# Hybrid decoder step in fp32 on one core: the last recurrent strip in an order of its own, and the first head of each half on a timetable that reaches into the next pass

## What is computed

```python
xn = rmsnorm(x, norm_mix)
xl, gl, q, k, v, z, b_raw, a_raw, u_pool, g_lru, g_dn, g_pool = split_cols(xn @ w_in)
h, h_last = rg_lru(causal_dwconv(xl, ...), ...)             # h[t] = a[t] * h[t-1] + b[t]
o_lru = h * gelu(gl)
o, s_last = gated_delta_rule(qh, kh, vh, beta, g, s0)       # 8 heads of 128, solves (I + A) X = B per chunk
o_dn = rmsnorm(o) * dn_norm_w * silu(z)
o_pool = multiscale_pool(u_pool, ...)
merged = (sigmoid(g_lru) * (o_lru @ w_br_lru) + sigmoid(g_dn) * (o_dn @ w_br_dn)
          + sigmoid(g_pool) * (o_pool @ w_br_pool))
x = x + merged @ w_out
x = x + square(relu(rmsnorm(x, norm_mlp) @ w_up)) @ w_down
```

## Time and profile before

| | |
|---|---|
| median of 3 runs | 2178.59 us |
| lowest, highest | 2177.43, 2178.78 us |
| profiled execution | 2176.55 us |
| its span, first to last instruction | 2174.8 us |
| TensorE busy | 2145.8 us, 99% of the span |
| VectorE, ScalarE, GpSimd busy | 1214.7, 771.8, 180.3 us |
| mean granted TensorE clock | 0.995 |

### The profile page before, as it was taken

The page is one execution under the profiler, slowest core; times in us unless marked ns, Lnnn a source line. Parts: engine busy times, 40 slices in busy tenths (PEclk is TensorE's granted clock), DMA queues, the critical chain, the costliest instruction groups (busy, mean ns, idle before and its releaser), DMA issues.

```text
span 2174.8 us, 34073 instructions
## 1 busy us (share of the span) xinstructions
PE 2145.8 (99%) x14515; PEld 2092.5 (96%) x14515; DVE 1214.7 (56%) x1996; ACT 771.8 (35%) x944; POOL 180.3 (8%) x340
## 2 busy tenths in 40 slices
PE   9999998999999999999999999999999999999997
PEld 9998997999998999999999999999999999999997
DVE  7996885555565655555545554444444444444444
ACT  6334552322232322333333443333333333333333
POOL 7000102110032110020000100000000000000001
PEclk9999999999999999999999999999999999999999
DMA  7443443334443343346444444545454444444443
GB/s 231 148 150 117 145 150 97 118 118 128 125 148 107 119 125 119 108 136 194 154 146 153 148 146 147 154 146 153 148 150 151 148 153 147 154 146 155 146 153 110
DMA packets 295638, 309.40 MB, mean 142 GB/s; under 512 B 9712, under 2 KB 290416, under 8 KB 295232
## 3 DMA queue, kind: packets, MB, share of 16 engines
q1 hardware_dynamic: 291616, 291.54, 43.0%
q0 software_dynamic: 3584, 15.55, 2.4%
q10 hardware_dynamic: 288, 0.15, 0.0%
HBM read 298.83 MB, written 8.37 MB: 141 GB/s over the span
## 4 chain that ended last, share of the span: by engine, by line
PE 88%; DVE 7%; ACT 2%; issue 1%; DMA 1%; SPq 0%; DVEq 0%; ACTq 0%
PE main L1432 27%; PE main L1434 26%; PE main L1433 26%; PE aux L1552 6%; DVE lo L887 2%; DVE scratch L887 2%; DVE scratch L894 1%; ACT hi L621 1%; DVE scratch L891 1%; DMA raw<-in_w_in 1%; PE aux L1525 0%; PE aux L1656 0%; PE aux L1535 0%; DVE qkv L894 0%; DVE merged L887 0%
## 5 line engine op out<-in xcount | busy, mean ns | idle before, releaser
L887 DVE TENSOR_TENSOR lo<-raw,hi 128x1024 fp32r<-128x1024 f32 x546 | 660.4, 1228 | 376.3 <-ACT hi L621 369.0
L1432 PE MATMUL main<-x_hi,hi 128*128 128x320 f32 x2688 | 842.4, 313 | 2.9 <-DVE x_lo L894 2.4
L1434 PE MATMUL main<-x_hi,lo 128*128 128x320 f32 x2688 | 831.4, 309 | 0.0
L1433 PE MATMUL main<-x_lo,hi 128*128 128x320 f32 x2688 | 831.2, 309 | 0.0
L621 ACT ACTIVATE hi<-raw 128x1024 fp32r<-128x1024 f32 x546 | 566.5, 1054 | 688.3 <-DMA raw<-in_w_up 220.4
L1432 PEld LDWEIGHTS main<-x_hi,hi 128*128 128x128 f32 x2688 | 505.5, 188 | 11.0 <-issue 5.0
L1433 PEld LDWEIGHTS main<-x_lo,hi 128*128 128x128 f32 x2688 | 505.6, 188 | 0.7
L1434 PEld LDWEIGHTS main<-x_hi,lo 128*128 128x128 f32 x2688 | 505.1, 188 | 0.0
L1432 PE MATMUL main<-o_hi,hi 128*128 128x320 f32 x1408 | 444.3, 316 | 4.6 <-DVE o_lo L887 4.6
L1434 PE MATMUL main<-o_hi,lo 128*128 128x320 f32 x1408 | 435.7, 309 | 0.0
L1433 PE MATMUL main<-o_lo,hi 128*128 128x320 f32 x1408 | 435.5, 309 | 0.0
(11 more groups left out here) (253 smaller groups left out, 1191.6 us busy)
## 6 DMA issues: line engine op xcount, KB each, us to landing
raw<-in_w_in SPq DMA_DIRECT2D x210, 512.0 KB, 3.5
raw<-in_w_up SPq DMA_DIRECT2D x128, 512.0 KB, 3.7
raw<-in_w_down SPq DMA_DIRECT2D x128, 512.0 KB, 3.4
raw<-in_w_back SPq DMA_DIRECT2D x80, 512.0 KB, 3.4
scratch<-in_s_in POOLq DMA_DIRECT2D x8, 512.0 KB, 4.9
out_s_out<-scratch POOLq DMA_DIRECT2D x8, 512.0 KB, 4.6
merged<-in_x SPq DMA_DIRECT2D x8, 320.0 KB, 7.6
qkv<-in_x POOLq DMA_DIRECT2D x1, 2560.0 KB, 12.4
```

The costliest lines, as they stand in the source:

```text
L887: return dve.tensor_tensor(out, a, b, op)
L1432: pe.matmul(bank, hi, xh, start=first, stop=False)
L1433: pe.matmul(bank, hi, xl, start=False, stop=False)
L1434: return pe.matmul(bank, lo, xh, start=False, stop=last)
```

## The change

Four edits, all in the order of work and in who does it:

1. The chain of strip 3 stands on VectorE behind the split of tile 3 in the order 3, 0, 4, 1, 5, 2, 6 with no split between, and step 7 (the split of the product) one tile later. ScalarE has its steps 0, 3, 1, 4, 2 behind the same tile and step 5 behind tile 5's split. The old step 5 of VectorE is cut in three (5, 6, 7), and the GELU of strip 3 has a buffer of its own (`GQ`).
2. The first head of each half has places of its own for all 19 steps, from tile 5, block 0 to block 3 of tile 0 of the next pass. On VectorE `merge` and `gate` stand at other places among its steps.
3. In every head ScalarE, not VectorE, makes `KBG` (three instructions of 128 columns), and no longer waits for `dn_lt`; VectorE makes `QKD` behind `dn_lt`, not ahead of it.
4. GpSimd prepares the rows of a half's first head ahead of clearing buffers (for head 0 ahead of `o_ready`), and stores `conv_out` earlier. The product of pooling group 3 stands one tile earlier on TensorE, two positions earlier on VectorE and ScalarE.

```diff
+        GQ = (G2, G2, G2, MG[:, 14 * N:16 * N])
...
             def half(h0):
-                rows(h0)
+                ch.link(pool.memset(DTM, 0.0))
+                pool.sem_inc(rm_ready, 1)
                 clear_rows()
...
             pool.wait_ge(row_beg, 2)
-            ch.link(pool.memset(DTM, 0.0))
+            rows(0)
+            pool.wait_ge(o_ready, 4)
             half(0)
...
         def dn_place(k, peeled):
-            if peeled and k < 14:
-                return ((5, 3), (6, 1), (6, 4), (6, 6), (7, 0), (7, 2), (7, 4), (7, 6), (7, 7),
...
+            if peeled:
+                after = (0, 6, 11, 14, 17, 21, 24, 28, 30, 33, 35, 38, 40, 43, 45, 48, 51, 54, 59)[k]
+                return 5 + after // 8, after % 8
...
# ScalarE, dn_step k == 1
-                    act.wait_ge(lt_ready, h + 1)
+                    for c, n in enumerate((P, P, NS)):
+                        act.activation(KBG[0:n, c * P:(c + 1) * P], AX[3][0:n, c * P:(c + 1) * P], ACT.Copy,
+                                       scale=cols(COL, h, 1, c * 56 + 48, 1, n))
...
-            gated(0, GPL_N, GPL_T, 0, lru_steps(lru_step, 3), True)
+            gated(0, GPL_N, GPL_T, 0, {4: [lambda k=k: lru_step(3, k) for k in (0, 3, 1, 4, 2)], 6: [lambda: lru_step(3, 5)]})
...
# VectorE, gated and late
+                    own = {8: [gate0], 9: [dn[0]], 10: [dn[1], dn[2]], 11: [dn[3], merge0, dn[4]], 12: [dn[5], dn[6]]}
...
+                    return {1: [dn[7], dn[8]], 2: [dn[9], dn[10], dn[11]], 3: [dn[12], gate1, dn[13], dn[14]],
+                            4: [dn[16]], 5: [dn[17], merge1, dn[18]]}
...
+            gated(0, GPL_N, GPL_T, 0, 0, 0, {4: [lambda k=k: lru_step(3, k) for k in (3, 0, 4, 1, 5, 2, 6)],
+                                            5: [lambda: lru_step(3, 7)]})
...
# TensorE, gated
+                    for h in (h0, it + h0) if it == 1 else (it + h0,):
+                        for k in range(19):
+                            j, b = dn_place(k, h == h0)
+                            j -= 12 * (it + h0 - h)
+                            if 0 <= j < 12:
+                                between[j] = list(between.get(j, ())) + [(b, lambda h=h, k=k: dn_step(h, k, first))]
...
-            gated(0, GPP_N, GPP_T, 4, 8, 4, {3: [(7, lambda: pool_product(3))]})
+            gated(0, GPP_N, GPP_T, 4, 8, 4, {2: [(7, lambda: pool_product(3))]})
```

More of the change, by code:

```diff
@@ L427, in lru @@
                 history(it + 12, it + 12, it * 2 + 24, it * 4 + (LRU_T + 2 + BANKS))
+                if it == 3:
+                    pool.wait_ge(tail_copied, 16)
+                    pool.dma_start(A["conv_out"], CO).then_inc(out_stored, 16)
                 pool.wait_ge(h_ready, it + 1)
@@ L442, in _ @@
                 lru(it)
-            pool.wait_ge(tail_copied, 16)
+            pool.wait_ge(out_stored, 16)
             pool.wait_ge(lho_copied, 4)
-            pool.dma_start(A["conv_out"], CO).then_inc(out_stored, 16)
             pool.dma_start(A["lru_out"], LHO[:]).then_inc(out_stored, 16)
-            pool.wait_ge(out_stored, 32)
-            pool.wait_ge(o_ready, 4)
             def rows(h):
@@ L456, in rows @@
                                              None, ALU.mult)
-                ins.then_inc(rm_ready, 1)
+                return ins
             def head(h, following):
@@ L468, in head @@
                 if following:
-                    rows(h + 1)
+                    rows(h + 1).then_inc(rm_ready, 1)
                 pool.wait_ge(dn_done, h + 1)
@@ L523, in _ @@
             pool.wait_ge(o_ready, 8)
-            ch.link(pool.memset(DTM, 0.0))
+            rows(4)
             half(4)
@@ L573, in lru_steps @@
             return {pos: [lambda k=k: step(it, k) for k in ks]
-                    for pos, ks in ((3, (0,)), (4, (1,)), (5, (2, 3)), (6, (4,)), (7, (5,)))}
+                    for pos, ks in ((3, (0,)), (4, (1,)), (5, (2, 3)), (6, (4,)), (7, (5, 6, 7)))}
         def qkv_steps(rms, silu, rows):
@@ L597, in dn_place, with dn_steps @@
             return (5 + (k - 6) // 2, (3, 7)[k % 2]) if k < 18 else (11, 6)
-        def dn_steps(step, h, peeled, late):
+        def dn_steps(step, h, late):
             steps = {}
             for k in range(19):
-                pos = dn_place(k, peeled)[0] + 4
+                pos = dn_place(k, False)[0] + 4
                 if (pos > 12) == late:
@@ L769, in dn_step, with gated @@
                     act.activation(S1, AX[2][:, 0:P], ACT.Copy).then_inc(s1_ready, 1)
[L771 to L774, removed]
+            def gated(it, n0, t0, h0, after):
+                if it == 0:
+                    own = {8: [lambda: gate(0, 0, t0, 0)], 10: [lambda: dn_step(h0, 0)], 11: [lambda: dn_step(h0, 1)]}
+                else:
+                    own = joined({8: [lambda: gate(it, 0, t0, 0)]}, dn_steps(dn_step, it + h0, False))
                 walk(split, n0, 12, it, 12, joined(after, own))
             def late(it, t0, h0):
-                steps = {2: [lambda: gate(it, 1, t0, 0)]}
-                return steps if h0 is None else joined(steps, dn_steps(dn_step, it + h0, False, True))
-            gated(0, GPL_N, GPL_T, 0, lru_steps(lru_step, 3), True)
+                if it == 0:
+                    return {3: [lambda: gate(0, 1, t0, 0)], 4: [lambda: dn_step(h0, 15), lambda: dn_step(h0, 16)]}
+                return joined({2: [lambda: gate(it, 1, t0, 0)]}, dn_steps(dn_step, it + h0, True))
+            gated(0, GPL_N, GPL_T, 0, {4: [lambda k=k: lru_step(3, k) for k in (0, 3, 1, 4, 2)], 6: [lambda: lru_step(3, 5)]})
             for it in range(1, 4):
@@ L1196, in dn_step @@
                     tt(XT[0:NS, NP:N], ident[0:NS, 0:NS], YY[0:NS, NP:N], ALU.subtract).then_inc(lt_ready, 1)
+                    for n, c, _ in both:
+                        tt(QKD[0:n, c], AX[1][0:n, c], DTM[0:n, c], ALU.mult)
                 elif k == 2:
@@ L1240, in dn_step, with gated @@
                     ins.then_inc(dn_done, 1)
[L1242 to L1245, removed]
+            def gated(it, n0, t0, g0, h0, branch, after):
+                gate0, merge0 = lambda: gate(n0, t0, it, 0), lambda: merge(n0, t0, g0, it, 0, branch)
+                dn = [lambda k=k: dn_step(h0, k) for k in range(19)]
+                own = {8: [gate0], 10: [merge0]}
+                if h0 is not None and it == 0:
+                    own = {8: [gate0], 9: [dn[0]], 10: [dn[1], dn[2]], 11: [dn[3], merge0, dn[4]], 12: [dn[5], dn[6]]}
+                elif h0 is not None:
+                    own = joined(own, dn_steps(dn_step, it + h0, False))
                 walk(split, n0, 12, it, 12, joined(after, own))
             def late(it, n0, t0, g0, h0, branch):
-                steps = {2: [lambda: gate(n0, t0, it, 1)], 4: [lambda: merge(n0, t0, g0, it, 1, branch)]}
-                return steps if h0 is None else joined(steps, dn_steps(dn_step, it + h0, False, True))
-            gated(0, GPL_N, GPL_T, 0, 0, 0, lru_steps(lru_step, 3), True)
+                gate1, merge1 = lambda: gate(n0, t0, it, 1), lambda: merge(n0, t0, g0, it, 1, branch)
+                dn = [lambda k=k: dn_step(h0, k) for k in range(19)]
+                if h0 is not None and it == 0:
+                    return {1: [dn[7], dn[8]], 2: [dn[9], dn[10], dn[11]], 3: [dn[12], gate1, dn[13], dn[14]],
+                            4: [dn[16]], 5: [dn[17], merge1, dn[18]]}
+                steps = {2: [gate1], 4: [merge1]}
+                return steps if h0 is None else joined(steps, dn_steps(dn_step, it + h0, True))
+            gated(0, GPL_N, GPL_T, 0, 0, 0, {4: [lambda k=k: lru_step(3, k) for k in (3, 0, 4, 1, 5, 2, 6)],
+                                            5: [lambda: lru_step(3, 7)]})
             for it in range(1, 4):
```

31 lines of the change are left out of this document (12 added, 19 removed).

## The result

| | before | after |
|---|---|---|
| median, 4 runs each in turn on one chip | 2178.69 us | 2156.24 us |
| lowest, highest | 2177.43, 2179.11 us | 2156.06, 2157.65 us |
| profiled execution | 2176.55 us | 2156.06 us |
| its span | 2174.8 us | 2154.3 us |
| mean granted TensorE clock | 0.995 | 0.997 |

The ratio is 0.990, with a 95% interval of 0.9889 to 0.9912: faster, by 22.4 us in the medians and 20.5 us between the two profiled spans. The forecast was 14.9 us.

The account below looks back on a forecast made before the run. TensorE, busy 99% of the span, was taken as the bound. Removing 12.6 us of waits and 5.1 us of clock loss (17.7), less 2.8 us of new waits, gave 14.9 us net: 2163.7 us, range 2160 to 2169.

Parts of the forecast that it names:

- Edit 1: Last strip's chain: o_lo ends at 333.5 us, so TensorE's 4.6 us wait and 1.7 us of clock go.
- k = 2: TensorE's two waits for dn_lt in each half's first head go: 5.0 us, plus 3.4 us of clock.
- The clock: TensorE's time at the lower clock behind the three long waits comes back: 5.1 us.
- The small waits: TensorE's waits at first heads' doublings and line 1200's copy in six other heads: 1.4 and 1.6 us go.
- The four of the doublings: Four TensorE waits at the doublings of the first heads, together 1.4 us, counted as gone.
- (a), the wait at k = 1: First half's first head: TensorE newly waits for VectorE's keys, 1.3 to 1.9 us, taken as 1.3.
- (b), k = 18: First head of each half: a new TensorE wait of 0.5 us, 1.0 in all.
- (c), the other handshakes: Remaining new places in the first heads: added TensorE waits, taken as 0.5 us in all.
- the clock that falls behind k = 1: Rival, 25%: TensorE's clock drops behind the new wait for the keys, costing 1.7 us; 2165.4 us.
- The late handshakes: Rival, 8%: longer VectorE tile splits delay first-head steps, 5 us plus 3.4 us of clock; 2172.1 us.
- the changed names: Rival, 7%: o_lo comes early but first heads wait 3 to 4 us a half instead; 2176 to 2179 us.
- the lasting low clock: Rival, 5%: waits at many first-head places keep TensorE's clock low, making the kernel slower; 2194 us.

Follow-up runs that it names:

- e5_edit3_all: Kernel before, with ScalarE making KBG without waiting for dn_lt and VectorE making QKD behind dn_lt, in all eight heads; 2168.92 us, ratio 0.9959.
- e1_six_heads: Kernel before, with ScalarE making KBG and VectorE making QKD behind dn_lt only in the six heads that don't begin a half; 2174.29 us, ratio 0.9983.
- e4_rows_early: Changed kernel, with GpSimd making head 0's rows ahead of its copies of the last states; 2157.38 us, ratio 0.9905.
- e6_rows_and_wait: Changed kernel, with head 0's rows made ahead of the last states' copies and ScalarE's wait for those copies moved to head 0's k = 0; 2155.00 us.
- e9_all: Changed kernel, with head 0's rows made early, ScalarE's wait for the copies moved, and k = 5 of six heads one block later; 2153.28 us, ratio 0.9888.
- e2_chain_alone: Kernel before, with only strip 3's chain in the new order and its own GELU buffer, GpSimd's order unchanged; 2175.03 us, ratio 0.9989.
- e8_k5_later: Changed kernel, with k = 5 of the six heads that don't begin a half moved one TensorE block later; 2155.44 us, ratio 0.9896.

## Why the prediction was wrong

The direction was right, and so was the mechanism of the long waits and their clock, but the time was not: 2156.24 us lies under the range of 2160 to 2169. The gain was 7.5 us larger than forecast. 1.9 of these are that the profiled execution before took 2176.55 us and its median 2178.69, while after the two are 0.2 apart (without them the time would still lie under the range); 0.6 are idle time (10.4 for 9.8); 5.0 stand neither in the idle rows nor in the clock: the hidden part of the waits, less what was lost elsewhere.

- **Edit 1: right.** VectorE after, from the scans to `o_lo`:

```profile
328.97 1.54 DVE L1119 TENSOR_TENSOR_SCAN scratch<-scratch 128x320 f32<-128x320 f32 x2
330.54 0.82 DVE L901 SCALAR_TENSOR_TENSOR scratch<-scratch 128x640 f32<-128x640 f32 x1
331.29 1.22 DVE L894 TENSOR_TENSOR lo<-raw,hi 128x1024 fp32r<-128x1024 f32 x1
332.42 0.82 DVE L894 TENSOR_TENSOR o_lo<-scratch,o_hi 128x640 fp32r<-128x640 f32 x1
```

  `o_lo` ends at 333.2, forecast 333.5, and the wait of 4.6 us is gone. On ScalarE the root follows its table load at once, as in the earlier trace rows; the drain of about 1380 ns that the Trainium skill (ScalarE: Activation LUTs, "What ACT_TABLE_LOAD costs") adds to a switch isn't seen after either:

```profile
325.38 1.28 ACT L720 ACT_TABLE_LOAD   x1
326.68 0.74 ACT L720 ACTIVATE scratch<-scratch 128x640 f32<-128x640 f32 x1
```

- **k = 2: right.** No wait at line 1594 and 5.0 us out. `e5_edit3_all` shows that edit 3 alone takes half of it and, in its profiled execution, all of its clock. The rest is put down to the further places of edit 2, which was not run alone.
- **The clock: right** in sum, 5.1 us back at the three places. "The clock was low only in four windows" leaves out the end of the program, where it was low as well, before and after.
- **The small waits: this is the step that failed.** "The four of the doublings (1.4 us)" and "I count 1.6 of 1.8 us" took as price what TensorE's rows show as idle, 3.0 us in all; by the starts they were worth 9.8. The six waits of line 1200 were worth 4.5 us by the starts (6.46 to 1.93) and 4.1 (1.7 to 5.7) as run alone in `e1_six_heads`. At the doublings of the first heads, k = 5 to 13, the steps cost 2.65 us a head by the starts where 0.73 are idle: 5.3 us for 1.4. Five of the seven steps that waited show no idle time at all, only a wait of the weight load; the two others, k = 10 and 13, cost 0.27 and 0.26 us more than their rows.
- **(a), the wait at k = 1: missed, and another came.** Forecast 1.3 us at k = 1, measured an excess of 0.06 there and a wait of 2.2 us at k = 0, where the text said that GpSimd costs nothing. TensorE after:

```profile
340.27 0.85 PE L1568 MATMUL aux<-head_rows,row_pickers 48*128 48x320 f32 x4 [2.20 <-POOLq L487]
343.81 1.37 PE L1568 MATMUL aux<-scratch 128*128 128x128 f32 x10
```

  GpSimd after, ahead of 340.27 (the store of the last states and a clear of 0.35 us are left out):

```profile
330.57 0.84 POOL L434 COPY lru_h_out<-scratch 128x1 f32<-128x1 f32 x1 [18.17 <-DVE scratch L1119]
331.36 1.20 POOL L435 COPY lru_h_out<-scratch 128x8 f32<-128x8 f32 x1
332.50 0.79 POOL L434 COPY lru_h_out<-scratch 128x1 f32<-128x1 f32 x1
333.23 1.20 POOL L435 COPY lru_h_out<-scratch 128x8 f32<-128x8 f32 x1
...
335.60 4.27 POOL L456 TENSOR_SCALAR head_rows<-rows_split,ident_pairs 48x320 fp32r<-48x320 f32 x2
```

  The copies end at 334.43. ScalarE's split of tile 6 waits for them, after:

```profile
334.46 2.01 ACT L624 ACTIVATE hi<-raw 128x1024 fp32r<-128x1024 f32 x2 [2.32 <-POOL lru_h_out L435]
```

  and VectorE's split waits for ScalarE's:

```profile
335.56 2.36 DVE L894 TENSOR_TENSOR lo<-raw,hi 128x1024 fp32r<-128x1024 f32 x2 [1.18 <-ACT hi L624]
343.23 0.48 DVE L894 TENSOR_TENSOR scratch<-scratch,aux 128x320 f32<-128x320 f32 x1
```

  So the copies hold both chains. The order of ScalarE shown for the change lists that wait (`lho_copied`), but the forecast's sum for the keys has no term for it; VectorE waits 1.18 us there. The late k = 0 covers the keys that were late too (they end at 343.23 + 0.48 = 343.7, forecast 342.9). `e4_rows_early` took one of the chains away and found the other, `e6_rows_and_wait` both. What the forecast called 1.3 us cost 2.3; the place was wrong.
- **(b), k = 18: right.** Forecast 0.5 us in each half, measured an excess of 0.62 in each, 0.36 of it shown as idle.
- **(c), the other handshakes: 0.5 us forecast**, about 0.3 measured, all excess at other steps of the two first heads added; in the second half there is no wait at k = 0 or 1 over 0.12 us, as forecast.

Of the rivals, the clock that falls behind k = 1 was not seen after, where nothing waits there. With a wait at k = 1 it fell in one of three: behind 2.1 us in `e4_rows_early` (0.66), not behind 0.86 us in `e6_rows_and_wait` and `e9_all` (1.00, with the same six transposes behind it). The late handshakes, the changed names and the lasting low clock did not come, though `e2_chain_alone` is the changed names in small: 4.6 us of `o_lo` turned into 3.3 us for the rows.

## What to carry to other kernels

Where TensorE is the bound, add up the waits of its weight loads, or the gaps between the starts of its matmuls, not the idle time of the matmuls: here a wait for a stationary operand cost 0.2 to 0.3 us more than its row, and steps without a row cost up to 0.35. When a step is moved forward, follow each of its partners back to its own last wait: a small copy on an idle engine held two chains. An edit that only removes one of two equal chains shows nothing, so take the second away before dropping the first.

## What the runs showed of the hardware that was not expected

**GpSimd's instructions grew beside VectorE's.** The same four copies before:

```profile
330.67 0.19 POOL L430 COPY lru_h_out<-scratch 128x1 f32<-128x1 f32 x1 [19.35 <-DVE scratch L1112]
330.79 0.20 POOL L431 COPY lru_h_out<-scratch 128x8 f32<-128x8 f32 x1
```

Then VectorE evacuated PSUM; after, it runs products and splits of two SBUF inputs from 330.54 on, and the copies take 0.84, 1.20, 0.79 and 1.20 us (the same in `e2_chain_alone`), four to six times as long. They end at 331.41, 332.56, 333.29 and 334.43, each some 0.05 us behind the end of a VectorE instruction (331.36, 332.51, 333.24 and 334.37, the last the split that starts at 333.16), while VectorE's split keeps its 1.22 us. (Not everywhere: the split at 343.63 us after takes 1.38, beside a product of GpSimd that takes 1.84 where before it took 0.87.) The rows (4.27 us for two) took 2.78 before. The Trainium skill (SBUF — State Buffer, "SBUF: two separate sides") says that the two engines share a pair of ports, held by one for a whole instruction while the other blocks. That fits these rows for the copies, but no kernel here measured the contention by itself, so it is argued from the traces and not shown.

**The clock does not fall by the length of a wait alone.** In the profiled executions it did not fall behind waits of 0.9 to 1.7 us in the heads (`e5_edit3_all`, `e6_rows_and_wait`, `e9_all`, `e2_chain_alone`). Behind 2.1 us (`e4_rows_early`), 2.15 and 2.8 (before, both k = 2), 3.3 (`e2_chain_alone`), 4.6 and 5.0 us it did. But behind 2.2 us it stayed at 1.00 after and fell to 0.54 and 0.78 in `e8_k5_later`, with the same work around it, and behind the 2.8 us of the second half it stayed at 1.00 in `e2_chain_alone` where before it was 0.66. The wait for `x_lo` at 9 us goes the same way: behind 1.9 us of it the clock fell in `e8_k5_later` (0.93 and 0.73 in the windows 5 to 10 and 10 to 15 us), behind 2.9 us in `e4_rows_early` it stayed at 1.00. What decides between 1.9 and 2.9 us stays open. It may be why the runs of before spread over 4 us in one batch (2175.48 to 2179.40) and those of `e9_all`, which has no such wait in the middle of the program, over 0.3. The mean clocks go with it (0.995 or 0.996 in the six fastest of those 21 runs of before, 0.993 or 0.994 in the eleven slowest), but with one trace for each kernel the place of the loss isn't shown.
